# Two of three dilated attention groups computed on even and odd tokens, diagonal blocks alone

## What is computed

```python
DIL_PAIRS = ((128, 1), (512, 4), (2048, 16))

for gi, (w, d) in enumerate(DIL_PAIRS):
    steps = jnp.arange(n_keys[gi]) * d
    idx = t[:, None] + w - steps[None, :]
    k_g = k_pads[gi][:, idx]
    v_g = v_pads[gi][:, idx]
    logits = jnp.einsum('bqhd,bqjhd->bhqj', q_c[:, :, gi], k_g,
                        preferred_element_type=jnp.float32) * scale + bias_g[gi][:, None, :]
    logits = jnp.where((t[:, None] - steps[None, :]) >= 0, logits, NEG_INF)
    lse = jax.nn.logsumexp(logits, axis=-1)
    p = jnp.exp(logits - lse[..., None]).astype(v.dtype)
    outs.append(jnp.einsum('bhqj,bqjhd->bqhd', p, v_g, preferred_element_type=jnp.float32))
    lses.append(lse)
wts = jax.nn.softmax(jnp.stack(lses, axis=0), axis=0)
out = sum(wts[gi].transpose(0, 2, 1)[..., None] * outs[gi] for gi in range(N_DIL))
```

## Time and profile before

| | us |
|---|---|
| median of 3 runs | 1002.76 |
| lowest and highest | 1002.12, 1002.85 |
| the profiled execution | 1001.44 |
| its span, first to last instruction | 999.7 |
| TensorE busy in the span | 983.8 |
| VectorE busy | 629.3 |
| ScalarE busy | 594.9 |

### The profile page before, as it was taken

The page is one execution under the profiler, slowest core; times in us unless marked ns, Lnnn a source line. Parts: engine busy times, 40 slices in busy tenths (PEclk is TensorE's granted clock), DMA queues, the critical chain, the costliest instruction groups (busy, mean ns, idle before and its releaser), DMA issues.

```text
span 999.7 us, 13330 instructions
## 1 busy us (share of the span) xinstructions
PE 983.8 (98%) x4920; PEld 791.9 (79%) x4920; DVE 629.3 (63%) x782; ACT 594.9 (60%) x929; POOL 12.2 (1%) x22
## 2 busy tenths in 40 slices
PE   7999999999999999999999999999999998999998
PEld 5888788888888777788888888877777776778877
DVE  5676775555556765675555557866757657776654
ACT  5777665454546655465454445776767576866571
POOL 1000000000000000000000000000000000000000
PEclk9999999999999999999999999999999999999999
DMA  8536265755563633556756663644344234336551
GB/s 275 172 115 210 77 199 200 240 174 204 170 208 127 210 127 127 168 175 226 252 192 228 210 206 131 210 168 169 126 135 157 86 127 156 111 112 213 205 173 43
DMA packets 106041, 170.26 MB, mean 170 GB/s; under 512 B 3988, under 2 KB 65302, under 8 KB 106000
## 3 DMA queue, kind: packets, MB, share of 16 engines
q1 hardware_dynamic: 103360, 161.23, 47.6%
q0 software_dynamic: 2304, 8.37, 2.6%
q10 hardware_dynamic: 336, 0.10, 0.0%
HBM read 168.58 MB, written 1.11 MB: 170 GB/s over the span
## 4 chain that ended last, share of the span: by engine, by line
PE 96%; ACT 2%; DVE 2%; issue 0%; DMA 0%; ACTq 0%; DVEq 0%
PE acc L434 14%; PE acc L436 13%; PE acc L435 13%; PE acc L485 12%; PE pair_ps L436 7%; PE pair_ps L434 7%; PE pair_ps L435 7%; PE acc L713 3%; PE acc L536 3%; PE turn_ps L609 2%; PE acc L630 2%; PE pair_ps L597 2%; PE acc L577 1%; PE pair_ps L596 1%; PE turn_ps L503 1%; PE turn_ps L434 1%
## 5 line engine op out<-in xcount | busy, mean ns | idle before, releaser
L1665 DVE TENSOR_TENSOR w_lo<-w_raw,w_hi 128x2048 fp32r<-128x2048 f32 (+2 forms) x155 | 345.5, 2232 | 127.4 <-ACT w_hi L1026 127.1
L1026 ACT ACTIVATE w_hi<-w_raw 128x2048 fp32r<-128x2048 f32 (+2 forms) x155 | 288.3, 1863 | 80.6 <-PE acc L436 35.5
L434 PE MATMUL acc<-w_hi,uT_hi 128*128 128x512 f32 (+3 forms) x552 | 221.3, 401 | 3.2 <-DVE w_lo L2096 2.6
L436 PE MATMUL acc<-w_hi,uT_lo 128*128 128x512 f32 (+3 forms) x552 | 212.8, 385 | 0.0
L435 PE MATMUL acc<-w_lo,uT_hi 128*128 128x512 f32 (+3 forms) x552 | 211.9, 384 | 0.0
L434 PEld LDWEIGHTS acc<-w_hi,uT_hi 128*128 128x128 f32 x552 | 104.1, 189 | 30.7 <-issue 9.2
L434 PE MATMUL pair_ps<-w_hi,uT_hi 128*128 128x512 f32 x320 | 126.5, 395 | 0.0
L436 PE MATMUL pair_ps<-w_hi,uT_lo 128*128 128x512 f32 x320 | 124.8, 390 | 0.0
L435 PE MATMUL pair_ps<-w_lo,uT_hi 128*128 128x512 f32 x320 | 124.6, 390 | 0.0
L436 PEld LDWEIGHTS acc<-w_hi,uT_lo 128*128 128x128 f32 x552 | 103.9, 188 | 21.2
L435 PEld LDWEIGHTS acc<-w_lo,uT_hi 128*128 128x128 f32 x552 | 104.4, 189 | 17.5
(11 more groups left out here) (230 smaller groups left out, 1233.4 us busy)
## 6 DMA issues: line engine op xcount, KB each, us to landing
w_raw<-in_w_in SPq DMA_DIRECT2D x46, 1024.0 KB
w_raw<-in_w_gate SPq DMA_DIRECT2D x44, 512.0 KB
w_raw<-in_w_up SPq DMA_DIRECT2D x44, 512.0 KB
w_raw<-in_w_down SPq DMA_DIRECT2D x22, 1024.0 KB
w_raw<-in_w_out SPq DMA_DIRECT2D x12, 1024.0 KB
w_raw<-in_w_qkv SPq DMA_DIRECT2D x16, 512.0 KB
w_raw<-in_w_branch SPq DMA_DIRECT2D x6, 1024.0 KB
bias<-rel_rows POOLq DMA_DIRECT2D x5, 1024.0 KB, 7.2
```

Source lines behind the costliest of these rows:

```text
L434: mm(o, xh, wh[:, k, :], start=first and k == 0, stop=False)
L436: done = mm(o, xl, wh[:, k, :], start=False, stop=last and k == len(kts) - 1)
L1026: activation(w_hi[:, slot, 0:width], w_raw[:, slot, 0:width], ACT.Copy).then_inc(hi_done, 1)
L1665: v.tensor_tensor(w_lo[:, slot, 0:width], w_raw[:, slot, 0:width], w_hi[:, slot, 0:width].bitcast(f32), ALU.subtract).then_inc(lo_done, 1)
```

## The change

In the dilated groups of steps 4 and 16 the two blocks of 128 are no longer tokens 0 to 127 and 128 to 255 but the even tokens and the odd ones.

- **Projection.** While those two groups are projected (`n.classes` is set), `half_unit` takes the stationary operand from every second column of `uT_hi` and `uT_lo`, starting at the block's number. The rows of queries, keys and values come out by parity. ScalarE scales them with `class_scale`, which POOL makes from the row scales by a store to DRAM and a load in the other order.
- **Attention** (kind `"classes"`). Query block 1 is multiplied with key block 1 alone. The logits of a pair are two diagonal blocks, 256 columns for a head instead of 384. There are four transposes of probabilities instead of six, and each product of values is 128 columns. VectorE adds the bias in two operations of 128 columns per head and takes all maxima in one, ScalarE's exponentials are all 128 wide, the copies of probabilities 256.
- **Bias.** The distances between tokens of one parity are even. POOL stores two more tables at the start, one of them with every second element of `rel_f`, and `rel_stored` counts to 48. The windows for the two groups are 128 columns from it.
- **Back to token order.** ScalarE's copy of a pair's output writes with a step of two, so that the output turns back in token order. Maxima and totals are kept by parity and go through DRAM once more (`class_stats`, `stat_rows`, `stats`); VectorE waits for them at the first gate.
- **Loops.** The loops of three turns on TensorE, ScalarE and VectorE are written out. SyncE's loop stays.

The diff, cut to its core:

```diff
+            pool.dma_start(class_rows[:, 0:P - 1], rel_f[16:32, 0:P - 1]).then_inc(rel_stored, 16)
+            pool.dma_start(class_rows[:, P - 1:S - 1], rel_f[16:32, P - 1:REL:2], allow_slow_non_contiguous=True)\
+                .then_inc(rel_stored, 16)
...
+            pool.wait_ge(row_scale, 6)
+            pool.dma_start(scale_rows.rearrange("(b p) -> p b", p=P), norms[:, LN2, 5, :], allow_slow_non_contiguous=True)\
+                .then_inc(scale_stored, 16)
+            pool.wait_ge(scale_stored, 16)
+            pool.dma_start(class_scale[:, :], scale_rows.rearrange("(p b) -> p b", b=TB)).then_inc(scale_full, 16)
             pool.wait_ge(max_done, 16)
             pool.dma_start(bias[:, 0, :, :], windows(rel_rows, 32 * REL, REL, 8)).then_inc(bias_full[4], 16)
             pool.wait_ge(bias_full[4], 16)
...
+            for i in range(2):
+                pool.wait_ge(class_kept, i + 1)
+                pool.dma_start(stat_rows[i].rearrange("(p b) c -> p b c", b=TB),
+                               class_stats[:, i, :, :, :].rearrange("p b k h -> p b (k h)")).then_inc(stat_stored, 16)
+                pool.wait_ge(stat_stored, 16 * (i + 1))
+                pool.dma_start(stats[:, i, :, :, :].rearrange("p b k h -> p b (k h)"),
+                               stat_rows[i].rearrange("(b p) c -> p b c", p=P)).then_inc(stat_full, 16)
...
+            def columns(x, kt, blk):
+
+                return x[:, kt, blk:S:TB] if n.classes else x[:, kt, tokens(blk)]
...
-                    xh, xl = x_hi[:, kt, tokens(blk)], x_lo[:, kt, tokens(blk)]
+                    xh, xl = columns(x_hi, kt, blk), columns(x_lo, kt, blk)
...
-                    done = mm(pair_ps[:, j, 128:384], q[:, 128:256], k, start=True, stop=True)
+                    if kind == "classes":
+                        done = mm(pair_ps[:, j, 128:256], q[:, 128:256], k[:, 128:256], start=True, stop=True)
+                    else:
+                        done = mm(pair_ps[:, j, 128:384], q[:, 128:256], k, start=True, stop=True)
...
-                    for i in range(3):
+                    for i in range(prob_width(kind) // P):
...
+                        if kind == "classes":
+                            done = mm(bank[HD * j:HD * j + HD, P * blk:P * blk + P], v,
+                                      prT[:, t % 2, j, P * blk:P * blk + P], start=True, stop=True, skip_group_check=True)
+                            continue
...
-            with pe.Fori(0, 3) as g:
-                n.unit, n.chunk, n.pair, n.turn = u0 + g * 6, c0 + g * 3, p0 + g * 4, t0 + g * 4
-                project_and_attend((512, 512, 512), "last", g * 2 + 3, g * 6 + 36)
-            n.unit, n.chunk, n.pair, n.turn = u0 + 18, c0 + 9, p0 + 12, t0 + 12
-            project_and_attend((512, 512, 256), "last", 9, 54)
+            for g in range(3):
+                project_and_attend((512, 512, 512), ("last", "last", "classes")[g], g * 2 + 3, g * 6 + 36,
+                                   classes=g > 0)
+            project_and_attend((512, 512, 256), "classes", 9, 54)
...
+                    dst, src = outs[t % 2], out_ps[:, 0:S]
+                    if kind == "classes":
+                        dst, src = by_class(dst), src.rearrange("p (c i) -> p c i", c=TB)
+                    activation(dst, src, ACT.Copy).then_inc(out_copied, 1)
...
+                if g == 1:
+                    act.wait_ge(scale_full, 16)
...
+            def class_maxima(t, pr, pair0, bias_of):
+
+                for blk in range(TB):
+                    cols = block_cols("classes", blk)
+                    done = v.scalar_tensor_tensor(pr[:, :, blk, ::-1], pair_ps[:, :, cols][:, :, ::-1], HD ** -0.5,
+                                                  bias_of(t), ALU.mult, ALU.add)
+                done.then_inc(logit_read, 1)
+                dve.wait_ge(logit_read, pair0 + (t + 1))
+                v.tensor_reduce(negmax8[:, :, 2 * t:2 * t + 2].rearrange("p b j -> p j b"), pr, op=ALU.max, axis=AX.X,
+                                negate=True).then_inc(max_done, 1)
...
-                dve.wait_ge(rel_stored, 16)
+                dve.wait_ge(rel_stored, 16 * 3)
...
+                    if head0 in (16, 24):
+                        i = head0 // 8 - 2
+                        v.tensor_copy(class_stats[:, i, :, 0, :], negmax8[:, :, :])
+                        v.tensor_copy(class_stats[:, i, :, 1, :], total8[:, :, :]).then_inc(class_kept, 1)
+                        return
...
                 gate_branch(0, 0)
+                dve.wait_ge(stat_full, 32)
```

More of the change, by code:

```diff
@@ L76, in build_program @@
     rel_rows = nc.dram_tensor("rel_rows", [40, REL], f32, kind="Internal").ap()
+    class_rows = nc.dram_tensor("class_rows", [16, S - 1], f32, kind="Internal").ap()
+    scale_rows = nc.dram_tensor("scale_rows", [S], f32, kind="Internal").ap()
+    stat_rows = [nc.dram_tensor(f"stat_rows{i}", [S, 16], f32, kind="Internal").ap() for i in range(2)]
     ctx = ExitStack()
@@ L119, in build_program @@
         tabT = sb("tabT", [32, 40])
+        class_scale = sb("class_scale", [P, TB])
         flat_bias = bias[:, :, :, :].rearrange("p a b c -> p (a b c)")
         flat_heads = heads[:, :, :, :].rearrange("p a b c -> p (a b c)")
+        class_stats, stats = [bias[:, 3, 0, 128 + 64 * i:192 + 64 * i].rearrange("p (g b k h) -> p g b k h", g=2, b=TB, k=2)
+                              for i in range(2)]
         flat_qkv = qkv[:, :, :, :].rearrange("p a b c -> p (a b c)")
@@ L235, in build_program, with by_class, block_cols, prob_width @@
         stored = sem("stored")
+        def by_class(x):
+            return x.rearrange("p (i c) -> p c i", c=TB)
+        def block_cols(kind, blk):
+            return slice(P * blk, P * blk + P) if kind == "classes" else key_cols(blk)[0]
+        def prob_width(kind):
+            return 256 if kind == "classes" else 384
         def since(e, s, v):
@@ L623, in values @@
                 bank = out_bank(kind, t)
-                if kind != "last":
+                if kind != "last" and kind != "classes":
                     since(pe, out_read, pair0 + t if bank is out_ps else pair0 + t - 1)
@@ L1123, in copy_pair @@
                 act.wait_ge(qkT_done, n.turn + 1)
-                if kind == "last":
+                if kind in ("last", "classes"):
                     activation(qkT[:, t, 0:S], qkT_ps[:, 0:S], ACT.Copy, scale=g_now[:, 0:1])
@@ L1165, in attention_step @@
                 if 2 <= s:
-                    copy_probs(s - 2, pair0)
+                    copy_probs(s - 2, pair0, kind)
             def project(chunks, early=0):
@@ L1582, in _ @@
             own0, s0, q0, r0 = own[0], n.sums, n.squares, n.roots
-            with act.Fori(0, 3) as g:
+            for g in range(3):
                 n.unit, n.chunk, n.pair, n.turn = u0 + g * 6, c0 + g * 3, p0 + g * 4, t0 + g * 4
@@ L1829, in attention_step @@
                 if 1 <= s < 5:
-                    copy_probs(s - 1, pair0)
+                    copy_probs(s - 1, pair0, kind)
             def band_mixer():
@@ L2133, in _, with class_table @@
                 dve.wait_ge(bias_full[g], 16)
-            u0, p0, own0, s0, q0, r0, k0 = n.unit, n.pair, own[0], n.sums, n.squares, n.roots, n.qk
-            with dve.Fori(0, 3) as g:
-                n.unit, n.pair, own[0] = u0 + g * 6, p0 + g * 4, own0 + g * 8
-                n.sums, n.squares, n.roots, n.qk = s0 + g * 2, q0 + g * 2, r0 + g * 2, k0 + g * 2
-                def table_g(t, cols):
-                    return flat_bias[:, bass.ds(g * 2048 + (2 * t * S), 2 * S)]\
-                        .rearrange("p (j c) -> p j c", j=2)[:, :, back(cols)]
-                project_and_attend(6, "last", g * 8, table_g, {1: head_sums, 3: head_sums},
-                                   after_unit={2: head_norm(0), 4: head_norm(1)})
-            n.unit, n.pair, own[0] = u0 + 18, p0 + 12, own0 + 24
-            n.sums, n.squares, n.roots, n.qk = s0 + 6, q0 + 6, r0 + 6, k0 + 6
+            def class_table(slot):
+                return lambda t: bias[:, slot, 2 * t:2 * t + 2, 0:P]
+            for g in range(3):
+                project_and_attend(6, ("last", "last", "classes")[g], g * 8, class_table(g) if g == 2 else table(g),
+                                   {1: head_sums, 3: head_sums}, after_unit={2: head_norm(0), 4: head_norm(1)})
             def swish_gate(i):
```

62 lines of the change are left out of this document (44 added, 18 removed).

## The result

| | before | after |
|---|---|---|
| median, us | 1002.44 (1001.78 to 1002.85, 4 runs) | 1010.33 (1008.68 to 1010.98, 4 runs) |
| profiled execution, us | 1001.44 | 1010.52 |
| its span, us | 999.7 | 1008.7 |
| TensorE busy, us | 983.8 | 981.5 |

The ratio is 1.0077, with a 95% interval of 1.0059 to 1.0094. TensorE is busy 2.3 us less, and the span is 9.0 us longer: the change put 11 us of waiting into the program. The page of the kernel after shows where to look; it answers to the earlier trace rows.

A forecast was written before the change was run, and what follows sets the result against it. TensorE was taken to bound the kernel; 2.6 us saved in the step 4 stretch plus 1.85 in step 16, all other terms zero, gave 4.5 us off 1002.76, or 998.3 us. Forecast 997.5 to 999.1, wider range 996.9 to 1001.0.

The forecast's parts named there:

- What bounds the kernel: Whole kernel: TensorE is 96% of the 999.7 us span, so only shrinking its own time counts.
- 0.66 us per pair: TensorE's logits, transposes and values for a pair of heads: 0.22 us saved in each, 5.3 us over eight pairs.
- All 2.6 us arrive in the step 4 stretch: Attention of step 4, 742.1 to 788.6 us: TensorE waits for nobody, so the whole 2.6 us saving shortens it.
- the sign of being wrong that I had set: Step 4 group: 43.9 us expected instead of 46.5; a span above 45 us would prove the prediction wrong.
- 1.85 us arrive in the step 16 stretch: Attention of step 16, 788.6 to 831.7 us: two waits swallow part of the saving, leaving 1.85 instead of 2.6 us.
- my first rival: All or nearly all of 5.3 us arrives, perhaps opening step 16's 1.4 us of waits: 996.1 to 997.5 us; chance 0.10.
- Strided stationary operand, zero: 288 projection products reading every second column: no cost at the same load rate, 2.4 us at half rate.
- Loops, row scales, statistics, zero: Written-out loops, and row scales and maxima and totals going through DRAM on POOL's queue: all hidden, zero cost.
- "Side work (1)", the element store, zero: Extra bias-row stores at the start: 2048 single elements take 23 us, hidden under some 46 us before VectorE's use.
- The rival with this store: Single-element store not spread: over 1300 us on one DMA engine, 1044 on four; decides from 46 us on; chance 0.03.

The follow-up runs named there:

- E8: E1 with, in the step 16 group, VectorE storing outputs ahead of weight splits and ScalarE copying probabilities ahead of rounding in the last two steps; 998.65 us.
- E2: E1 with the two class groups' projections reading 128 neighbouring tokens instead of every second one, so no longer attention within one parity; 998.66 us.
- E5: The kernel before with only the loops of three turns on TensorE, ScalarE and VectorE written out; 1001.88 us.
- E9: The changed kernel with the strided store of 2048 single elements issued from ScalarE's queue instead of POOL's; 1007.91 us.
- E1: The changed kernel with VectorE first packing every second bias element, so the store moves 16 runs of 512 bytes; 1000.47 us.
- E6: The changed kernel with the strided store made from the DRAM copy of the table after the first mixer, issued at 126.89 us; 1009.75 us.
- E4: The changed kernel with only the first 64 of the 128 strided columns stored as single elements, the rest contiguously; 1005.05 us.
- E10: The changed kernel with only the first 32 of the 128 strided columns stored as single elements, the rest contiguously; 999.3 us.

## Where the prediction was right and where it failed

- **What bounds the kernel**: right, TensorE. But "a microsecond counts only where TensorE's own time shrinks" left out the other half: it also counts where something makes TensorE wait.
- **0.66 us per pair**: right, 0.64. 0.20, 0.23 and 0.21 us for the three pieces.
- **All 2.6 us arrive in the step 4 stretch**: 2.6 less 0.6 for the operand and 0.4 for a new wait at ScalarE's copy. I had looked at probabilities as the only thing that could be late. The group's 44.96 us are 0.04 below the sign of being wrong that I had set.
- **1.85 us arrive in the step 16 stretch**: 1.33 in the kernel after. The wait ahead of the outputs' turn grew from 1.19 to 1.63 us as it should, since VectorE's chain stands still while TensorE gets ahead. Two waits of 0.4 us for ScalarE's copies are new there as well. It was the order of two helpers, and E8 brings 3.25 us there: 2.6 of pieces and the 1.4 of old waits, less these two. That the old waits could go was in my first rival, though by shorter work and not by another order.
- **Strided stationary operand, zero**: failed, 1.2 us (E2). The argument was that a load of 188 ns overlaps its neighbours and needs at most 0.11 us of a pitch of 0.23, so that a few ns more would be hidden. They are not: 6 to 7 ns more in the load, 4 ns more in the pitch of every product. It is inside the bounds that I gave (0 to 2.4). The Trainium skill, Advanced Engine Details and Errata, SBUF Cachelines, has two accesses to a line of 16 bytes at full rate; this trace shows 3% less than that.
- **Loops, row scales, statistics, zero**: right, the loops by E5, the others by the trace of the kernel after. The first gate doesn't wait for the statistics: VectorE's L2289 runs at 869.21, right behind L2279, and TensorE waits nowhere for the scales.
- **"Side work (1)", the element store, zero: this is the step that failed, and it made the sign wrong.** The landing time came near, 23 us estimated and 26.2 measured, but by luck: my 0.18 us per packet is the mean of 2304 packets with 8.37 MB, 3.6 KB each, and nothing in it is a price of a single element of 4 bytes. What was asked of the time failed outright: I compared it with the 46 us until VectorE's first use behind `rel_stored` and stopped there, as if only those who wait for a transfer could be hurt by it. Those who share the 16 engines with it were not looked at: the weight units, with 13 us of cover. The rival with this store ("it decides from 46 us on") was about the right instruction with the wrong point of decision, since it too reckoned from the semaphore. The point lies where a weight unit in flight takes longer than 13 us, at somewhere between 512 and 1024 elements. The same section of the Trainium skill that I read for the spread, DMA: Bandwidth & Descriptors, Rules for kernel authors, says that a strided last dimension becomes one descriptor per element; E9's 2064 packets agree. That was the warning, and I took from it only that they are spread.

In sum: 997.5 to 999.1 was forecast and 1010.33 came. With the store packed (E1) it is 1000.47, and with the helpers' order put right (E8) 998.65, within the forecast, for reasons of which one, the order, was not in it.

## What to carry to other kernels

Ask of every new transfer not only who waits for it but what else is in flight on the same DMA engines while it runs, and compare its length with the cover of that stream, here 13 us of prefetch. Pack strided elements on a compute engine before they are stored: one small copy on VectorE was worth 9 to 10 us. When TensorE gets faster in a place where it already waits, look at the order on the helpers: an operation that is ready should not stand behind one that still waits.

## What was not expected of the hardware

- 8 KB stored as 2048 single elements takes 21.5 to 26.2 us, and 5.1 us as 16 contiguous rows. While it runs, a weight unit of 576 KB, 3.6 us in the kernel before, takes 20.6 to 24.8 us, and one of 1 MB 21.7. It is so from POOL's queue and from ScalarE's, from SBUF and from DRAM (E6), and at two places of the program.
- In such a stretch the DMA share goes up and the GB/s go down (0.72 and 19 against 0.40 and 118), since each weight packet takes longer (0.62 us on the mean against 0.09). The two columns have to be read together.
- A stationary operand with a step of two float32 loads in 194 to 195 ns instead of 188, and the pitch of products with 512 columns grows by 4 ns although the load has room in it.
- The same wait of 1.62 to 1.63 us was followed by a granted clock at the 1.2 GHz level in three profiled executions (E1, E2, E4) and not in four others (after, E6, E9, E10).
